# Two transformer-like blocks in one fp32 kernel: the memory's keys and values moved to the front, RWKV tiles into the S5 loop

## The reference

```
silu_c = silu(c);  silu_cc = silu(c_ctx)
for l in (0, 1):                                  # first block
    mx = split(silu_c @ w_mod[l] + b_mod[l], 6)   # 1024 x 6144 matrix, mc alike from silu_cc
    zx = modulate(rms_norm(x, norm1_g[l]), mx[0], mx[1]) @ w_in[l]
    ...                                           # attention, Fourier and conv mixing, MLP
x = rms_norm(x, final_norm_g)
mem_n = rms_norm(mem, norm_mem)                   # second block; depends on mem alone
p_rw, p_s5, p_gla, p_gate = split(rms_norm(x, norm_mix) @ w_in_2)   # 1792, 512, 1552, 3072 columns
y_rw  = rwkv7_mix(p_rw)      # p_rw is first mixed with itself one token back, weights rw_mu
y_s5  = s5_mix(p_s5)         # complex diagonal state space, scan over the 256 tokens
y_gla = gla_mix(p_gla)       # chunked gated linear attention, 4 chunks of 64
x = x + (sum of sigmoid(p_gate) * branch(y)) @ w_out
q = rms_norm(x, norm_xattn) @ wq
k, v = split(mem_n @ wkv)                         # 1024 x 2048 matrix; depends on mem alone
x = x + softmax(q k / 16) v @ wo
x = x + conv_ffn(rms_norm(x, norm_ffn))
return rms_norm(x, norm_final)
```

## Time and profile before

| what | value |
| --- | --- |
| median of three runs | 1893.41 us (1891.93 to 1896.64) |
| the profiled execution | 1894.65 us, its span 1892.9 us |
| TensorE busy | 1788.5 us, 94% |
| VectorE busy | 926.6 us, 49% |
| ScalarE busy | 399.6 us, 21% |
| GpSimd busy | 278.1 us, 15% |
| moved by DMA | 256.22 MB, mean 135 GB/s |
| chain that ended last | 82% on TensorE, 11% on VectorE |

### The profile page before, as it was taken

The page is one execution under the profiler, slowest core; times in us unless marked ns, Lnnn a source line. Parts: engine busy times, 40 slices in busy tenths (PEclk is TensorE's granted clock), DMA queues, the critical chain, the costliest instruction groups (busy, mean ns, idle before and its releaser), DMA issues.

```text
span 1892.9 us, 25921 instructions
## 1 busy us (share of the span) xinstructions
PE 1788.5 (94%) x10456; PEld 1401.8 (74%) x10456; DVE 926.6 (49%) x1738; ACT 399.6 (21%) x757; POOL 278.1 (15%) x290
## 2 busy tenths in 40 slices
PE   5999998999999998898999899999999899999997
PEld 1344444888888886568999788774688688788886
...
GB/s 326 269 201 136 348 139 67 67 89 111 134 111 89 86 80 102 67 68 132 161 176 161 196 151 133 73 133 89 161 65 90 75 193 134 90 154 146 148 153 111
DMA packets 38416, 256.22 MB, mean 135 GB/s; under 512 B 4096, under 2 KB 7168, under 8 KB 8608
## 3 DMA queue, kind: packets, MB, share of 16 engines
...
q10 hardware_dynamic: 576, 4.19, 0.5%
...
HBM read 247.27 MB, written 7.34 MB: 135 GB/s over the span
## 4 chain that ended last, share of the span: by engine, by line
PE 82%; DVE 11%; ACT 2%; issue 2%; DMA 1%; POOL 1%; SPq 0%; ACTq 0%; DVEq 0%; POOLq 0%
PE ps L576 81%; DVE arena L1821 1%; DMA ring<-weights 1%; PE ps L740 1%; DVE arena L1977 1%; DMA cs_raw<-c_t 1%; POOL aux L1614 0%; DVE aux L1849 0%; DVE arena L1850 0%; DVE arena L1851 0%; ACT hT L1266 0%; DVE ring L1892 0%; DVE aux L1760 0%; DVE aux L1764 0%; DVE aux L1761 0%
## 5 line engine op out<-in xcount | busy, mean ns | idle before, releaser
L576 PE MATMUL ps<-hT,ring 128*128 128x256 f32 (+3 forms) x3184 | 739.0, 391 | 24.6 <-issue 17.0
L576 PEld LDWEIGHTS ps<-hT,ring 128*128 128x128 f32 (+1 forms) x3184 | 574.9, 194 | 177.7 <-issue 103.7
L576 PE MATMUL ps<-arena,ring 128*128 128x256 f32 (+3 forms) x1756 | 351.8, 356 | 4.3 <-DVE arena L1851 3.2
L576 PEld LDWEIGHTS ps<-arena,ring 128*128 128x128 f32 (+1 forms) x1756 | 293.6, 190 | 52.8 <-issue 11.7
L576 PE MATMUL ps<-arena,sums 128*128 128x256 f32 (+1 forms) x768 | 136.5, 327 | 1.3 <-DVE aux L1915 1.3
L576 PEld LDWEIGHTS ps<-arena,sums 128*128 128x128 f32 x768 | 118.2, 191 | 12.3 <-DVE aux L1915 2.5
L1604 POOL TENSOR_TENSOR aux<-aux 128x256 f32<-128x256 f32 (+1 forms) x40 | 42.5, 1062 | 553.8 <-ACT aux L1221 486.1
L1221 ACT ACTIVATE aux<-xT 128x256 f32<-128x256 f32 (+1 forms) x64 | 30.9, 494 | 282.6 <-DVE xT L2007 93.3
L1614 POOL TENSOR_SCALAR aux<-aux,small 128x512 f32<-128x512 f32 (+1 forms) x48 | 70.8, 1482 | 114.7 <-DVE small L1867 114.4
L576 PE MATMUL ps<-hT,sums 128*128 128x128 f32 (+1 forms) x512 | 78.6, 301 | 0.7 <-DVE aux L1915 0.4
L1633 POOL TENSOR_TENSOR arena<-arena 128x256 f32<-128x256 f32 (+1 forms) x32 | 27.0, 843 | 332.6 <-ACT arena L1383 332.6
...
## 6 DMA issues: line engine op xcount, KB each, us to landing
...
arena<-kept_turns POOLq DMA_DIRECT2D x6, 512.0 KB, 4.6
...
```

The lines of the kernel that those rows point to most:

```text
L576: ins = nc.tensor.matmul(o_, lhsT, rhs, start=start, stop=stop, skip_group_check=True)
```

## The change

The memory's part moves to the front. SyncE issues a small first part of the tables, `c`, the vectors, `mem` in two halves, and then weights; `ctx`, `x` and the rest of the tables come behind chunk 11. TensorE sums the memory's squares, and then takes the memory's keys and values between the first four blocks of w_mod. They lie in `spare` and GpSimd writes them to DRAM right away. The squares of `x` are summed by GpSimd, so that TensorE needs two matmuls for the first norm and not eight. In the second block `gkd` goes first, the GLA inputs next, and the RWKV tiles go in a new order (`RW_ORDER`): two before the S5 loop and twelve in it, followed by three gate tiles. GpSimd turns back all 16 states. VectorE's turn keeps its results in the PSUM bank it reads, so that the scan reads PSUM, and a small memset at its end hands the bank back. VectorE mixes one RWKV tile per step. The computation is the same.

```diff
-RW_CUTS = (5, 8, 11)
+X_CHUNK = 12
+RW_ORDER = (12, 13, 4, 5, 6, 7, 0, 1, 2, 3, 8, 9, 10, 11)
+RW_FIRST = 2
...
-SUM_ORDER = (1, 2, 3, 4, 6, 7, 8)
-SUMMED = {1: 7, 2: 6, 3: 7, 4: 6, 6: 7, 7: 7, 8: 7}
+SUM_ORDER = (0, 1, 2, 3, 4, 6, 7, 8)
+SUMMED = {0: 7, 1: 7, 2: 6, 3: 7, 4: 6, 6: 7, 7: 7, 8: 7}
...
-    for q in range(MOD_FIRST):
-        mod(0, q)
...
+    mod(0, 0)
+    keys(0, 2)
+    mod(0, 1)
+    keys(2, 6)
+    mod(0, 2)
+    keys(6, 8)
+    values(0)
+    mod(0, 3)
+    values(1)
...
+            open_bank(("mst", 0), "hold")
+            for k in range(KD):
+                pe.wait_ge(S["mem_squares"], k + 1)
+                mm(bank(("mst", 0))[:, 0:T], ones, memsq[:, k, :], k == 0, k == KD - 1, ("mst", 0) if k == KD - 1 else None)
...
+            pe.wait_ge(S["silu_c"], 2)
+            mod_block(0, 0)
+            mem_keys(0, 2)
+            mod_block(0, 1)
+            mem_keys(2, 6)
+            mod_block(0, 2)
+            mem_keys(6, 8)
+            mem_values(0, 0, KD)
             for k in range(KD):
                 norm_stat_step(("st", 0), 0, k, slice(0, 2 * T))
-            pe.wait_ge(S["silu_c"], 2)
-            for q in range(MOD_FIRST):
-                mod_block(0, q)
+            mod_block(0, 3)
+            mem_values(1, 0, 2)
             mod_turn(0, 0)
+            mem_values(1, 2, KD)
+            pe.wait_ge(S["tables_loaded"], 16)
...
+            plain("gkd", 0, 0, ("gkd", 0), m=16, ready=lambda k: pe.wait_ge(S["h2_ready"], k + 1))
             for n in range(8):
-                plain("glain", 0, n, ("glain", n), ready=(lambda k: pe.wait_ge(S["h2_ready"], k + 1)) if n == 0 else None)
-            for n in range(4):
-                plain("glago", 0, n, ("glago", n))
-            plain("gkd", 0, 0, ("gkd", 0), m=16)
-
-            taken(pe, ("gkd", 0))
-            for n in range(2):
...
             for n in range(S5T):
-                if n < KD:
-                    mem_key(n)
                 s5_out(n)
                 if n + 2 < S5T:
                     s5_in(n + 2)
-                if n >= KD:
-                    mem_value(*divmod(n - KD, 4))
+                if RW_FIRST + n < 14:
+                    rw_tile(RW_FIRST + n)
+                elif RW_FIRST + n < 14 + GATE_EARLY:
+                    gate_tiles(1)
 
             pe.wait_ge(S["rw_squash"], 2)
...
+            square_sum(0, slice(0, 2 * T))
+            for half in range(2):
+                for tt_ in range(2):
+                    taken(pool, ("xv", half, tt_))
+            pool.dma_start(kept, spare[:, :, :]).then_inc(S["mem_kept"], 16)
+            pool.wait_ge(S["mem_kept"], 16)
...
-                if j == 3:
-                    if g < 2:
-                        s5_turned_back(pool, n)
-                        pool.wait_ge(S["s5_states"], 3 * (g + 1))
-                        turns_back(g + 2)
-                    continue
...
-                did(tt(s_t1[:, :, :], bu, cos_[:, j:j + 1, :].to_broadcast([P, 2, T]), ALU.mult), wait=False)
-                did(tt(s_t2[:, :, :], bu, sin_[:, j:j + 1, :].to_broadcast([P, 2, T]), ALU.mult), key=key)
-                did(tt(s_t1[:, 0, :], s_t1[:, 0, :], s_t2[:, 1, :], ALU.add), wait=False)
-                did(tt(s_t1[:, 1, :], s_t1[:, 1, :], s_t2[:, 0, :], ALU.subtract))
+                did(tt(s_t2[:, :, :], bu, sin_[:, j:j + 1, :].to_broadcast([P, 2, T]), ALU.mult))
+                did(tt(bu, bu, cos_[:, j:j + 1, :].to_broadcast([P, 2, T]), ALU.mult))
+                did(tt(bu[:, 0, :], bu[:, 0, :], s_t2[:, 1, :], ALU.add), wait=False)
+                did(tt(bu[:, 1, :], bu[:, 1, :], s_t2[:, 0, :], ALU.subtract))
                 if n >= 2:
                     s5_turned_back(dve, n - 2)
                 mag = q[1][:, n:n + 1].to_broadcast([P, T])
                 for part in range(2):
-                    did(v.tensor_tensor_scan(s_w[n % 2][:, part, :], mag, s_t1[:, part, :], 0.0, ALU.mult, ALU.add),
+                    did(v.tensor_tensor_scan(s_w[n % 2][:, part, :], mag, bu[:, part, :], 0.0, ALU.mult, ALU.add),
                         "s5_scanned", wait=part == 1)
-                if j == 3:
-                    w, st = s_w[n % 2], s_s[n % 2]
-                    did(tt(s_t1[:, :, :], w[:, :, :], cos_[:, j:j + 1, :].to_broadcast([P, 2, T]), ALU.mult), wait=False)
-                    did(tt(s_t2[:, :, :], w[:, :, :], sin_[:, j:j + 1, :].to_broadcast([P, 2, T]), ALU.mult))
-                    did(tt(st[:, 0, :], s_t1[:, 0, :], s_t2[:, 1, :], ALU.subtract), wait=False)
-                    did(tt(st[:, 1, :], s_t1[:, 1, :], s_t2[:, 0, :], ALU.add), "s5_states_v")
+                did(v.memset(small2[:, 18, 0:1], 0.0), key=key)
+                if n < 14:
+                    rw_tile(n)
                 if n in (4, 8):
                     gla_end(n // 4 - 1)
...
-            dve.wait_ge(S["mem_kept"], 16)
...
+            sp.dma_start(tab[:, 0:NTAB_FIRST], table_in[:, 0:NTAB_FIRST]).then_inc(S["first_loaded"], 16)
+            sp.dma_start(cs_raw[:, :, :], c_in).then_inc(S["first_loaded"], 16)
+            sp.dma_start(vec[:, :], vectors).then_inc(S["first_loaded"], 16)
+            for i in range(2):
+                sp.dma_start(memn[:, 4 * i:4 * i + 4, :], mem_in[:, 4 * i:4 * i + 4, :]).then_inc(S[f"mem_loaded{i}"], 16)
+            for c in range(SLOTS):
+                sp.dma_start(ring[:, c, :, :], weights[c, :, :, :]).then_inc(landed[c], 16)
+            for c in range(SLOTS, X_CHUNK):
+                sp.wait_ge(chunks_used, c - SLOTS + 1)
+                sp.dma_start(ring[:, c % SLOTS, :, :], weights[c, :, :, :]).then_inc(landed[c % SLOTS], 16)
             sp.dma_start(xT[:, :, 0:T], ctx_in).then_inc(S["x_loaded"], 16)
             sp.dma_start(xT[:, :, T:2 * T], x_in).then_inc(S["x_loaded"], 16)
-            sp.dma_start(tab[:, :], table_in[:, 0:NTAB]).then_inc(S["small_loaded"], 16)
-            sp.dma_start(vec[:, :], vectors).then_inc(S["small_loaded"], 16)
-            sp.dma_start(cs_raw[:, :, :], c_in).then_inc(S["small_loaded"], 16)
-            n_first = min(SLOTS, n_chunks)
-            for c in range(n_first):
-                sp.dma_start(ring[:, c, :, :], weights[c, :, :, :]).then_inc(landed[c], 16)
-
-            with sp.Fori(1, n_chunks // SLOTS) as i:
+            sp.dma_start(tab[:, NTAB_FIRST:], table_in[:, NTAB_FIRST:NTAB]).then_inc(S["tables_loaded"], 16)
+
+            with sp.Fori(X_CHUNK // SLOTS, n_chunks // SLOTS) as i:
                 for c in range(SLOTS):
                     sp.wait_ge(chunks_used, i * SLOTS + (c - SLOTS + 1))
                     sp.dma_start(ring[:, c, :, :], weights[i * SLOTS + c, :, :, :]).then_inc(landed[c], 16)
```

293 lines of the change are left out of this document (153 added, 140 removed).

## The result

The changed kernel takes 1884.33 us (median of 4 runs, 1882.14 to 1885.55); beside it on the same chip the kernel before took 1894.05 (4 runs, 1891.93 to 1896.64). The ratio is 0.9944, with an interval from 0.9928 to 0.9959: 7.8 to 13.6 us less. The forecast was 16 less. The profiled execution has a span of 1880.3 us where the one of before had 1892.9: 12.6 less.

What follows compares the result with a forecast made beforehand. TensorE, busy 94% of the span, was taken as the bound. Opening +37.0, first z tile and second block's savings and new wait made -24.1; the loop's +8.1 gave -16.0, so 1878 us, range for 8 in 10 1867 to 1893.

Steps and rivals of the forecast that it cites:

- the forecast's rule: S5 loop: of VectorE's RWKV pair and GpSimd's turn back, whoever is first holds the other up; the pair costs 2.05 us.
- No meetings: Rival, S5 loop: pair and turn back pass each other, VectorE's step 4.6, loop waits 7.2, 1871 us; chance 0.19.
- PSUM writes: Rival, S5 loop: VectorE's in-place turns and scans in PSUM cost double, step 8.0, 1907 us; chance 0.07.
- GpSimd first: Rival, S5 loop: VectorE waits for both GpSimd products, step 6.95, about 28 us of waits, 1892 us; chance 0.20.
- The first projection at 81.5: Opening: with the memory's part in front, the first projection starts at 81.5, 37.0 us later; bounds 78 and 88.
- the memory's norm then ends at about 11.6: Opening: step placing the end of the memory's norm at about 11.6 us, after the load of `mem` and ScalarE's squares.
- the allowance for the cold tile and late weights: Opening: 2.5 us on top of 79.0, for half of a cold tile and 0.8 for late weights.
- What goes: First z tile -2.0; second block -55.2 memory, -0.9 norm matmuls, -3.5 root wait, -0.5 `gkd`, +1.0 new wait.
- The wait for the root: Second block: TensorE's wait on a `hold` bank, held by the memory's norm and emptied late by ScalarE, goes: -3.5 us.
- the new wait: Second block: 1.0 us at the first `s5_out`, its bank coming free after ScalarE's root; bounds 0 and 2.
- The loop: S5 loop: VectorE's step 5.75 leaves no slack, so GLA ends are paid nearly in full; 13.8 us of waits, +8.1.
- Behind the gate tiles: Part after the gate tiles, behind the S5 loop: forecast 0 us of change.

Runs made afterwards that it cites:

- forced in all: The changed kernel with one more memset ahead of the RWKV pair in each of 14 loop steps, putting VectorE behind GpSimd: 1885.92 us, ratio 0.9955.
- warmed runs: The changed kernel with nine extra ones-table matmuls ahead of the sum of the memory's squares: 1881.88 us; the same matmuls in two combined versions: 1865.12 and 1869.11 us.

## Why the prediction was right, and where it was off

*The mechanism and its sign hold.* The time lies in the range for 8 in 10; it is just outside the forecast's own range of 1873 to 1884, and the gain between medians is 9.7 us where 16 were forecast. The RWKV pair and GpSimd's turn back meet in each step. Of the 13 pairs that meet GpSimd's turn back, VectorE is first in seven (by 0.01 us): GpSimd's first product waits for it, and the second RWKV instruction for the product. In three pairs GpSimd is first, because ScalarE's copy of the tile is late (1267.96 against 1268.43); in two that copy comes so late, behind a long wait, that the pair meets only GpSimd's sums. The last is the instruction of 3.12, which the forecast's rule does not give: it costs the pair some 1.9 us more than the 2.05 that I summed, one step ahead of the first GLA end. VectorE's step is 5.54 (5.75 forecast), and TensorE's two long waits stand at steps 5 and 9. "No meetings" is refuted by the row of 1.37 us; "PSUM writes" by 0.70 and 0.43 for instructions that write it. "GpSimd first" happened in those three only, and when forced in all was worth waits of 14.1 in place of 28.

*The first projection at 81.5: 84.96, the largest miss (+3.5).* The step that failed is "the memory's norm then ends at about 11.6". I let the sum end with ScalarE's squares, which do end at 11.1, and put TensorE's own time at nothing. Its 16 records begin at 9.09; at the full pace of 0.22 they would end at 12.6, and TensorE, idle until then, took 0.40 for each and ended at 15.5. The warmed runs show what the idle time does: the sum takes 4.0 to 4.4 us in the three traces with warming, 5.3 to 6.6 in the ten without. I had given a cold tile 1.7 us, in the wrong place: the key tiles ran at full pace. `x` came 7 us later than forecast (12.7 us after its issue at 44.43, behind `ctx` and weights), which made the wait on GpSimd 2.26, not 0.4; the allowance for the cold tile and late weights, 2.5 in all, happened to cover that.

*What goes: -62.0 against -59.1.* The wait for the root is gone (-3.5, hit), the new wait is 0.86 (1.0 forecast). A memory tile was priced at 3.45 us; the traces show 3.50 to 3.58, about 1 of the 2.9. The other 2 are slow matmuls. Before, three tiles behind the root's wait took 12.49 us (granted clock 0.85) and three ahead of it 13.25 (0.80), where three take 10.5 at full pace; now only one such stretch is left, 12.22 (0.86), with an `s5_in` of 2.07 in place of 1.13 ahead of it. That is 4.7 us of slow matmuls before and 2.6 now. The sum had no term for them.

```profile
1203.43 13.25 PE L576 MATMUL ps<-hT,ring 128*128 128x256 f32 x48
...
1225.43 12.49 PE L576 MATMUL ps<-hT,ring 128*128 128x256 f32 x48
```

*The loop: +9.7 against +8.1.* Waits are 5.7 more than before, not 8.1: I took 13.8 for what was 11.4; VectorE's step is 0.2 shorter than forecast, and over 14 steps that is more than the difference. Missing in the sum is what follows a long wait: 7.3 us of slow matmuls, of which the kernel before already had 3.4. So the loop's sum is near by some luck: waits 2.4 too high and slow matmuls 3.9 left out have opposite signs. I had the row for it, used it for the opening and not for the loop.

*Behind the gate tiles: +1.6*, forecast 0. One tile ran slower with the same waits ahead of it; why its clock fell there now and not before stays open.

*The two rules of the Trainium skill.* The trace agrees with "SBUF — State Buffer", section "SBUF: two separate sides": a VectorE instruction with two SBUF inputs and one of GpSimd exclude each other for their full length (1.37 in place of 0.48; 0.48 again once one input is PSUM). That the one that starts first gets the ports, as the section says, the meetings bear out except the one of 3.12. With "VectorE: DVE Perf Modes", section "The TRN2 errata", no run here agrees: 512 columns with a PSUM input take 0.69 to 0.70, sums of 256 columns 0.43 with PSUM against 0.42 in SBUF; the rule asks for 62 cycles (120 less 58) between them.

What stays open: the median gain (9.7) is smaller than the profiled pair's (12.6), within the interval; the scatter of the first block is enough for that but was not traced run by run.
